# Two ways to spread PEER gates over an expert table: indirect accumulating DMAs for the first 128 tokens, one-hot products for the other 128

## The chip, the cores and the metric

The kernel runs on one core of one Trainium2 chip. The metric is device time in microseconds (us), the median of several executions. TensorE (PE in the profile) multiplies, VectorE (DVE) and ScalarE (ACT) do elementwise work, GpSimd (POOL) does elementwise work and issues DMAs of its own, and SyncE (SP) issues most DMAs. Weight loads of TensorE stand as PEld beside its products.

## The reference

The program runs a two-layer hybrid block (feed-forward, mixer, feed-forward) and then a second two-layer block (mixer, PEER) on 256 tokens of width 1024. The change is in PEER. Its core:

```python
q = (xt @ wq).reshape(T, 8, 2, 128)
s1 = einsum('thd,nd->thn', q[:, :, 0], k1); s2 = einsum('thd,nd->thn', q[:, :, 1], k2)
v1, i1 = top_k(s1, 16); v2, i2 = top_k(s2, 16)
cand = (v1[..., :, None] + v2[..., None, :]).reshape(T, 8, 256)
cidx = (i1[..., :, None] * 128 + i2[..., None, :]).reshape(T, 8, 256)
sc, pos = top_k(cand, 16)
eidx = take_along_axis(cidx, pos, axis=-1)        # 8 x 16 experts of a token
gate = softmax(sc, axis=-1)                        # per head
out[t] = sum over (h, k) of gate * gelu(u_tab[eidx] . x[t]) * v_tab[eidx]
```

There are 128 x 128 = 16,384 experts. Of a token's 128 choices two heads can name the same expert, and then both gates count.

## The kernel before

Weights come in units of 512 KB (128 partitions x 1024 floats). SP loads each into one of three slots of `ring`. ACT copies a unit to the rounded high part (`wsp`, line 435), and DVE subtracts to get the low part (line 438); three products of high and low parts stand for one full-precision product. POOL can make the low part in DVE's place (line 661). Semaphores order everything: a load waits for the low part three units back, a high part for the product three units back (`unit_done`), a product for its low part (`low_done`).

PEER of each layer gathers no rows. It computes all 16,384 activations for all 256 tokens and weights them with a dense table of gates, zero where an expert isn't chosen:

- Stage "U": `U_FIRST` = 62 of the 128 units of `u_tab`, each one product of 24 matmuls (line 688). ACT's gelu puts each into `arena`, and SP copies it out to `acts_dram`. In the meantime DVE selects: per token block b and head, `top16` on two score rows of 128, the 256 pair sums, `top16` on these, then the look-up of the chosen indices, and the softmax with ACT's exponential. DVE does nothing else in this stage, so POOL makes the low parts of `POOL_LOWS` = 60 units.
- Stage "selT": indices and gates of both blocks are transposed on TensorE.
- Stage "U2": the remaining 66 units. Behind each, from the second on, one group of four tokens: DVE writes one-hot rows for both index halves (line 2428) and multiplies the gates in (line 2437), TensorE multiplies the one-hots (eight matmuls, line 1285) into a 128 x 128 table of gates for each token, and ACT moves that to `arena`. `GROUPS` = 64 groups cover 256 tokens.
- Stage "V": `arena` holds the gates, and the activations come back from DRAM (`back`, four buffers, line 508). DVE multiplies them in (line 2455), ACT and DVE split the result (lines 1702 and 2466), and TensorE accumulates it against 128 units of `v_tab` (12 matmuls each, line 752). Before its first unit stand eleven matmuls whose result isn't used (`busy_bank`, line 678).

The order of each engine's instructions is written out by hand; there is no scheduler. `h` is saved to DRAM before the selection and comes back on POOL's queue after the last group (line 663), with the rows of the layer norm (lines 596 and 597).

Of the kernel before, what the change touches and what calls it, by code (L numbers as in the profile page):

```python
# [13 lines left out]
F32 = mybir.dt.float32  # L14
# [7 lines left out]
P = 128  # L22
# [20 lines left out]
U_FIRST = 62  # L43
POOL_LOWS = 60
SPILLED = 126
OH_SLOTS = 3
GATE_SCALE = 2.0 ** 15
GROUPS = T // 4
# [14 lines left out]
Q_N = Q_K1 + 256  # L63
# [18 lines left out]
PEER_STAGES = [("xT", 8, 0), ("tt", 16, 16), ("score", 4, 0), ("U", U_FIRST, U_FIRST), ("selT", 2, 0),  # L82
# [28 lines left out]
def build_program(nc, x, stream, consts, consts1, levels, p1, p2, swt, wa, wgu, rows1, rows2, rows3, out):  # L111
    ctx = ExitStack()
    with ctx:
# [28 lines left out]
        selT = at("selT", place + 8192 + 4 * 1280, [P, 4, T], F16)  # L142
# [7 lines left out]
        acts = at("acts", place, [P, 4, T])  # L150
# [145 lines left out]
        gates = arena[:, :].rearrange("p (j t) -> p j t", j=NKEYS)  # L296
# [23 lines left out]
        acts_dram = nc.dram_tensor("acts_dram", (NKEYS, P, T), F32, kind="Internal").ap()  # L320
# [8 lines left out]
        gated_last = sem("gated_last")  # L329
# [75 lines left out]
        def spills(slot):  # L405

            return len([j for j in range(U_FIRST, SPILLED) if j % 4 == slot])
# [62 lines left out]
        def _(sp):  # L470
# [24 lines left out]
            def act_out(U, j, q, it=0):  # L495

                U.freed(sp, q, (UNITS_BODY // 4) * it)
                if j < U_FIRST:
                    sp.dma_start(acts_dram[bass.ds(it * UNITS_BODY + j, 1)].rearrange("a p t -> p (a t)"),
                                 arena[:, bass.ds(it * (UNITS_BODY * T) + j * T, T)]).then_inc(acts_out, 16)  # L500
                else:
                    sp.dma_start(acts_dram[j], acts[:, j % 4, :]).then_inc(acts_slot[j % 4], 16)

            def act_back(l, j, it=0):

                if j >= 4:
                    sp.wait_ge(gated, SPILLED * l + j - 3 + it * UNITS_BODY)
                sp.dma_start(back[j % 4], acts_dram[bass.ds(it * UNITS_BODY + j, 1)].rearrange("a p t -> p (a t)"))\
# [3 lines left out]
            for l in range(DEPTH):  # L512
# [4 lines left out]
                with sp.Fori(0, full) as it:  # L517
                    for q in range(UNITS_BODY):
                        load(U.u + ahead + q, it, UNITS_BODY)
                        act_out(U, q, q, it)  # L520
                for q in range(full * UNITS_BODY, SPILLED):
                    load(U.u + ahead + q)
                    if q < U_FIRST:
                        act_out(U, q, q)
                    else:
                        act_out(U2, q, q - U_FIRST)
# [7 lines left out]
                sp.wait_ge(unit_done, V.u)  # L534
                act_back(l, 2)
# [2102 lines left out]
```

## Time and profile before

| | us |
|---|---|
| median of 3 runs | 3037.62 (3034.58 to 3039.28) |
| the profiled execution, its own time | 3034.38 |
| its span | 3032.6 |
| PE busy in it | 2990.2 (99%) |
| DVE busy | 2162.4 (71%) |
| ACT busy | 1493.2 (49%) |
| POOL busy | 416.6 (14%) |

Busy time is the sum over an engine's instructions. Some matmul records can be missing from a trace, and matmuls overlap in their pipeline, so of TensorE the distance from one group's start to the next's is read rather than durations. The 1.8 us between the span and the execution's own time lie outside the traced instructions.

### The profile page before, as it was taken

What the parts mean: (1) busy time and instruction counts of PE and PEld (TensorE: products, weight loads), DVE (VectorE), ACT (ScalarE), POOL (GpSimd) and SP (SyncE); (2) the same over time, 40 slices, a digit from 0 to 9 for tenths busy, and PEclk for the clock granted to TensorE, in tenths of its full rate; (3) what the DMA queues carried; (4) which work ended last, traced back from release to release, by engine and by line L of the source; (5) the groups of instructions that cost most, each with busy time, mean ns of one, the idle gap of its engine ahead of it and who ended that gap; (6) DMA issues with size and microseconds to landing.
All of it is one profiled execution on the core that took longest, in us unless ns stands there. A gap on an engine that the chain in (4) does not pass through costs nothing.

```text
span 3032.6 us, 55438 instructions
## 1 busy us (share of the span) xinstructions
PE 2990.2 (99%) x19048; PEld 2669.8 (88%) x19048; DVE 2162.4 (71%) x3762; ACT 1493.2 (49%) x2358; POOL 416.6 (14%) x246
## 2 busy tenths in 40 slices
PE   8999999999999999999999999999999999999998
PEld 7889888888898888899999988888899999988887
DVE  6677576766756667659777677776759967767776
ACT  4455444444645444444455555555444455545554
POOL 0001000000011002028800000001118810000000
PEclk9999999999999999999999999999999999999999
DMA  6543255555423554457766677775447776677775
GB/s 226 187 162 122 91 166 187 168 190 188 140 98 125 187 187 143 165 176 226 227 199 195 214 244 242 241 242 180 164 157 226 225 210 197 194 243 241 241 240 189
DMA packets 213017, 579.47 MB, mean 191 GB/s; under 512 B 23744, under 2 KB 88544, under 8 KB 212368
## 3 DMA queue, kind: packets, MB, share of 16 engines
q1 hardware_dynamic: 209504, 563.67, 58.2%
q0 software_dynamic: 3376, 13.94, 1.5%
q8 instruction: 90, 1.47, 0.2%
q14 instruction: 47, 0.39, 0.0%
HBM read 541.34 MB, written 36.18 MB: 190 GB/s over the span
## 4 chain that ended last, share of the span: by engine, by line
PE 91%; DVE 4%; ACT 2%; issue 2%; DMA 1%; POOL 0%; SPq 0%; ACTq 0%; DVEq 0%
PE acc L752 32%; PE work L688 31%; PE work L698 9%; PE work L700 4%; PE acc L1151 3%; PE acc L816 3%; PE acc L1285 2%; DVE wsp L438 1%; ACT wsp L435 1%; PE work L1185 1%; PE work L953 1%; PE work L967 1%; ACT scratch L1365 1%; PE work L1073 0%; DVE xsp L1773 0%
## 5 line engine op out<-in xcount | busy, mean ns | idle before, releaser
L438 DVE TENSOR_TENSOR wsp<-ring,wsp 128x1024 fp32r<-128x1024 f32 x824 | 1004.1, 1227 | 491.3 <-ACT wsp L435 490.5
L435 ACT ACTIVATE wsp<-ring 128x1024 fp32r<-128x1024 f32 x944 | 984.5, 1052 | 553.2 <-PE work L688 325.9
L688 PE MATMUL work<-xsp,wsp 128*128 128x256 f32 x7872 | 986.6, 286 | 2.0 <-DVE xsp L1776 2.0
L688 PEld LDWEIGHTS work<-xsp,wsp 128*128 128x128 f32 x7872 | 959.3, 193 | 4.8 <-DVE xsp L1776 2.4
L752 PE MATMUL acc<-wsp,hsp 128*128 128x512 f32 x4128 | 955.9, 390 | 6.4 <-issue 3.9
L752 PEld LDWEIGHTS acc<-wsp,hsp 128*128 128x128 f32 x4128 | 769.4, 188 | 170.3 <-issue 6.2
L698 PE MATMUL work<-xsp,wsp 128*128 128x512 f32 x1408 | 501.4, 399 | 7.1 <-DVE xsp L1773 5.4
L700 PE MATMUL work<-xsp,wsp 128*128 128x256 f32 x1408 | 395.1, 281 | 0.0
L698 PEld LDWEIGHTS work<-xsp,wsp 128*128 128x128 f32 x1408 | 264.5, 188 | 74.0 <-DVE xsp L1773 6.5
L661 POOL TENSOR_TENSOR wsp<-ring,wsp 128x1024 fp32r<-128x1024 f32 x120 | 305.9, 2557 | 156.8 <-ACT wsp L435 156.4
L1702 ACT ACTIVATE hsp<-arena 128x256 fp32r (+1 forms) x256 | 107.1, 419 | 354.4 <-PE acc L752 339.5
L700 PEld LDWEIGHTS work<-xsp,wsp 128*128 128x128 f32 x1408 | 265.9, 189 | 3.1
L563 POOL TENSOR_TENSOR st<-st,mhalf 128x1 f32<-128x1 f32 x24 | 20.5, 861 | 1573.5 <-DVE st L1793 803.9
L2428 DVE TENSOR_TENSOR one_hots<-iota,selT 128x512 f16<-128x512 f16 x256 | 97.1, 422 | 98.1 <-PE acc L1285 98.0
L2466 DVE TENSOR_TENSOR hsp<-arena,hsp 128x256 fp32r<-128x256 f32 x256 | 108.8, 425 | 57.1 <-ACT hsp L1702 57.1
L1400 ACT ACTIVATE hsp<-scratch 128x256 fp32r<-128x256 f32 x88 | 36.8, 418 | 218.3 <-DVE scratch L1866 218.3
L1392 ACT ACTIVATE scratch<-scratch 128x256 f32<-128x256 f32 x88 | 36.8, 418 | 186.5 <-DVE scratch L1856 186.5
L2455 DVE TENSOR_TENSOR arena<-arena,back 128x256 f32 (+1 forms) x252 | 105.2, 418 | 15.3 <-DMA back<-acts_dram 15.3
L2437 DVE TENSOR_TENSOR one_hots<-one_hots,selT 128x512 f16<-128x512 f16 x256 | 96.6, 419 | 0.0
L816 PE MATMUL acc<-wsp,xsp 128*128 128x512 f32 x384 | 96.0, 399 | 0.0
L1151 PE MATMUL acc<-wsp,xsp 128*128 128x512 f32 x384 | 94.0, 397 | 0.0
L1151 PEld LDWEIGHTS acc<-wsp,xsp 128*128 128x128 f32 x384 | 70.3, 188 | 15.4
(341 smaller groups left out, 2290.2 us busy)
## 6 DMA issues: line engine op xcount, KB each, us to landing
ring<-in_stream SPq DMA_DIRECT2D x944, 512.0 KB, 3.4
back<-acts_dram SPq DMA_DIRECT2D x252, 128.0 KB, 3.1
acts_dram<-acts SPq DMA_DIRECT2D x128, 128.0 KB, 3.6
acts_dram<-arena SPq DMA_DIRECT2D x124, 128.0 KB, 4.0
rows_sb<-in_rows POOLq DMA_DIRECT2D x10, 512.0 KB, 7.0
h_saved_dram<-h POOLq DMA_DIRECT2D x2, 1024.0 KB, 5.0
h<-h_saved_dram POOLq DMA_DIRECT2D x2, 1024.0 KB, 6.8
scratch<-in_levels POOLq DMA_DIRECT2D x3, 448.0 KB, 4.5
```

The costliest lines, as they stand in the source:

```text
L435: self.eng.activation(dst[:, 0, :], src, ACT.Copy).then_inc(high_done, 1)
L438: self.eng.tensor_tensor(dst[:, 1, :], src, dst[:, 0, :].bitcast(F32), ALU.subtract)\
L661: pool.tensor_tensor(dst[:, 1, :], ring[:, n % RING, :], dst[:, 0, :].bitcast(F32), ALU.subtract) .then_inc(low_done, 1)
L688: mm = pe.matmul(out_, lhsT=w[:, a, 128 * c:128 * c + 128], rhs=xsp[:, b, c, :], start=(c == 0 and n == 0), stop=(c == DC - 1 and n == 2))
L698: pe.matmul(out_, lhsT=w[:, 0, 128 * c:128 * c + 128], rhs=xcs[:, c, :, :].rearrange("p s t -> p (s t)"), start=(c == 0), stop=False)
L700: mm = pe.matmul(out_[:, 0:T], lhsT=w[:, 1, 128 * c:128 * c + 128], rhs=xsp[:, 0, c, :], start=False, stop=(c == DC - 1))
L752: mm = pe.matmul(ACC[2 * b + n][:, :], lhsT=act[:, pa, 128 * b:128 * b + 128], rhs=w[:, pw, 512 * n:512 * n + 512], start=(first and m == ...
L816: mm = pe.matmul(ACC[2 * (g % 2) + b][:, :], lhsT=xsp[:, px, c, 128 * b:128 * b + 128], rhs=w[:, pw, 512 * cc:512 * cc + 512], start=(c == ...
L1151: mm = pe.matmul(ACC[2 * (g % 2) + b][:, :], lhsT=xsp[:, px, c, 128 * b:128 * b + 128], rhs=w[:, pw, 512 * cc:512 * cc + 512], start=(c == ...
L1702: act.activation(hsp[:, j % 2, 0, :], arena[:, bass.ds(it * (6 * T) + j * T, T)], ACT.Copy)\
L2455: tt(a, a, back[j % 4], ALU.mult).then_inc(gated, 1)
L2466: tt(hsp[:, j % 2, 1, :], arena[:, bass.ds(it * (12 * T) + j * T, T)], hsp[:, j % 2, 0, :].bitcast(F32), ALU.subtract).then_inc(act_low, 1)
```

## The change

`U_FIRST` becomes 92, `POOL_LOWS` 18, `GROUPS` 32. `acts_dram` is replaced by a DRAM table for each layer, `second_dram`, of 128 x 128 x 256 floats. Of each unit's 256 columns the last 128 get the second block's activations; the first 128 get the first block's gates:

- In the mixer of the first block POOL clears the first block's half with 16 DMAs per layer, each 128 x 8 x 128 floats.
- DVE works out the position of each of the first block's choices (`spots`), and POOL adds the gates there with 128 indirect DMAs per layer, one for each head and rank, 128 single floats each. After the 16 of a head it waits until they have landed.
- The first block's activations stay in `arena`, the second block's go to `second_dram`. The second block's gates are made with one-hots as before, 32 groups behind units 92 to 123, and stand in `arena`. What comes back in stage V is therefore gates for the first block and activations for the second, and the same product serves both.
- The selection is done in three parts (four heads of the first block, its other four, the second block), with low parts of weights between them from unit 21 on.
- The last units of U2 have no group, `busy_bank` is gone, and gates and stages for V's first units stand between the last units of U2.

```diff
-U_FIRST = 62
-POOL_LOWS = 60
-SPILLED = 126
+U_FIRST = 92
+POOL_LOWS = 18
+EXP_AT = (19, 39, 76)
+ZEROED = 16
-GROUPS = T // 4
+GROUPS = P // 4
+ROUND = 16 * TOPK
...
+            to_clear = second_dram[l].rearrange("(r k p t) o -> r p k (t o)", r=ZEROED, p=P, t=T)
+            for r in range(ZEROED):
+                pool.dma_start(to_clear[r][:, :, 0:P], back0[:, 0:P].unsqueeze(1).broadcast_to([P, NKEYS // ZEROED, P]))\
+                    .then_inc(zeroed, 16)
...
+                pool.wait_ge(zeroed, 16 * ZEROED * (l + 1))
+                for i in range(PH):
+                    if i % (PH // 2) == 0:
+                        pool.wait_ge(ev("sel_ready"), 3 * l + i // (PH // 2) + 1)
+                    if PH * l + i:
+                        pool.wait_ge(scattered, ROUND * (PH * l + i))
+                    for n in range(TOPK * i, TOPK * i + TOPK):
+                        pool.indirect_dma_start(out=second_dram[l], in_=selv[:, 0, 2, n:n + 1], in_offset=None,
+                                                out_offset=bass.IndirectOffsetOnAxis(spots[:, n:n + 1], 0),
+                                                compute_op=ALU.add).then_inc(scattered, 16)
+                pool.wait_ge(scattered, ROUND * PH * (l + 1))
                 pool.wait_ge(g_done, GROUPS * (l + 1))
                 pool.dma_start(h, saved).then_inc(h_back, 16)
+                for s in range(4):
+                    pool.wait_ge(acts_slot[s], 16 * (l + 1) * spills(s))
                 load_rows(rows2[2 * l + 2, 0], rows2[2 * l + 2, 1])
...
-                    if q == SPILLED - 1:
+                    if q == NKEYS - 6:
                         sp.wait_ge(acts_out, 16 * U_FIRST * (l + 1))
-                        sp.wait_ge(ev("sel_ready"), NB * (l + 1))
-                        act_back(l, 0)
-                        act_back(l, 1)
+                        sp.wait_ge(scattered, ROUND * PH * (l + 1))
+                        second_back(l, 0)
+                        second_back(l, 1)
+                for q in range(NKEYS - 2, NKEYS):
+                    act_out(U2, l, q, q - U_FIRST)
+                sp.wait_ge(unit_done, V.u)
+                second_back(l, 2)
+                second_back(l, 3)
+                load(U.u + ahead + NKEYS - 2)
+                load(U.u + ahead + NKEYS - 1)
                 for s in range(4):
                     sp.wait_ge(acts_slot[s], 16 * (l + 1) * spills(s))
...
                 G = Group(part, "V")
-                busy_bank(G, 0, 11)
                 pe.wait_ge(g_moved, GROUPS * (l + 1))
...
-                    U2.free(act.activation(acts[:, q % 4, :], U2.bank(i)[:, 0:T], ACT.Gelu), i)
+                    act.activation(arena[:, q * T:q * T + P], U2.bank(i)[:, 0:P], ACT.Gelu)
+                    U2.free(act.activation(acts[:, q % 4, :], U2.bank(i)[:, P:T], ACT.Gelu), i)
+                    if q == NKEYS - 2:
+                        stage(0)
...
                 split.next = U.u + 3 + POOL_LOWS
                 dve.wait_ge(low_done, split.next)
+                for i in range(PH // 2, PH):
+                    for m in range(2):
+                        low_next()
+                        first_choice(0, i, m)
+                    if i == PH // 2:
+                        gates_of(0, 0, PH // 2)
...
+                for i in range(PH // 2, PH):
+                    low_next()
+                    second_choice(0, i, low_next if i % 2 else None)
+                low_next()
+                places(PH // 2, PH // 2)
+                for m in range(2):
+                    low_next()
+                    look_up(0, PH // 2, PH // 2, m, lambda: None)
+                spots_of(PH // 2, PH // 2)
+                less_the_first(0, PH // 2, PH // 2)
```

On DVE the selection of the first block's fifth head began in the kernel before without a low part between its instructions (its `top16` follows the last of the fourth head's). Now the first half ends with the spots, and from there each `top16` has a low part of a weight ahead of it (line 444 of the changed kernel is line 438 of before). The rows of the changed kernel at the end of the first half:

```order
L2452 COPY gmx<-rows_sb 128x4
L2453 TENSOR_TENSOR rows_sb<-rows_sb,gmx 128x64
L2469 SCALAR_TENSOR_TENSOR rows_sb<-rows_sb 128x64
L2470 TENSOR_SCALAR spots<-rows_sb,pr_75 128x64
L444 TENSOR_TENSOR wsp<-ring,wsp 128x1024
L2380 MAX topv<-acc 128x8
L2381 MAX_INDEX topi<-topv,acc 128x8
L2382 MATCH_REPLACE rows_sb<-topv,acc 128x128
L2385 MAX topv<-rows_sb 128x8
L2386 MAX_INDEX topi<-topv,rows_sb 128x8
L444 TENSOR_TENSOR wsp<-ring,wsp 128x1024
L2380 MAX topv<-acc 128x8
```

In the kernel before the first block's selection ended like this, and the second block's followed with no low part:

```order
L2391 COPY gmx<-rows_sb 128x8
L2392 TENSOR_TENSOR rows_sb<-rows_sb,gmx 128x128
L2345 MAX topv<-scores 128x8
L2346 MAX_INDEX topi<-topv,scores 128x8
L2347 MATCH_REPLACE rows_sb<-topv,scores 128x128
```

So low parts of weights have moved in between the selection's instructions on DVE.

On TensorE, at the end of U2 in the kernel before (line 688 is a unit's product, 1285 a group's, 678 the eleven unused matmuls, 752 stage V):

```order
L1285 MATMUL acc<-one_hots 128x128 [waits g_moved,oh_ready]
L1285 MATMUL acc<-one_hots 128x128 x7
L688 MATMUL work<-xsp,wsp 128x256 [waits low_done,bank_free3]
L688 MATMUL work<-xsp,wsp 128x256 x23
L678 MATMUL work<-xsp 128x512 [waits bank_free0]
L678 MATMUL work<-xsp 128x512 x10
L752 MATMUL acc<-wsp,hsp 128x512 [waits low_done,act_low,g_moved]
```

And in the changed kernel (714, 1310 and 778 are the same three lines):

```order
L1310 MATMUL acc<-one_hots 128x128 [waits g_moved,oh_ready]
L1310 MATMUL acc<-one_hots 128x128 x7
L714 MATMUL work<-xsp,wsp 128x256 [waits low_done,bank_free0]
L714 MATMUL work<-xsp,wsp 128x256 x23
L714 MATMUL work<-xsp,wsp 128x256 [waits low_done,bank_free1]
L714 MATMUL work<-xsp,wsp 128x256 x23
L714 MATMUL work<-xsp,wsp 128x256 [waits low_done,bank_free2]
L714 MATMUL work<-xsp,wsp 128x256 x23
L778 MATMUL acc<-wsp,hsp 128x512 [waits low_done,act_low,g_moved]
```

Three units now lie between the last group and stage V, and the unused matmuls are gone.

On POOL, the end of the low parts and the scatters of a layer (the last rows are h and the norm's rows coming back):

```order
L674 TENSOR_TENSOR wsp<-ring,wsp 128x1024 [waits high_done]
L682 DMA second_dram<-rows_sb,spots 4194304x1 [waits sel_ready,zeroed]
L682 DMA second_dram<-rows_sb,spots 4194304x1 x15
L682 DMA second_dram<-rows_sb,spots 4194304x1 [waits scattered]
L682 DMA second_dram<-rows_sb,spots 4194304x1 [waits scattered,sel_ready]
L687 DMA h<-h_saved_dram 128x2048 [waits g_done,scattered]
L608 DMA rows_sb<-in_rows 128x1024 [waits acts_slot2,acts_slot3,acts_slot1,acts_slot0]
```

These rows are new between the low parts and the return of h; the return now waits for the scatters too.

## Rows read from the trace of the kernel before

**Rows 1.** The page: busy time of the engines, and the group of ACT's high parts

```profile
PE 2990.2 (99%) x19048; PEld 2669.8 (88%) x19048; DVE 2162.4 (71%) x3762; ACT 1493.2 (49%) x2358; POOL 416.6 (14%) x246
...
L435 ACT ACTIVATE wsp<-ring 128x1024 fp32r<-128x1024 f32 x944 | 984.5, 1052 | 553.2 <-PE work L688 325.9
```

**Rows 2.** Chain that ended last, second layer's PEER: start, us, engine, line, instructions

```profile
2264.39 178.56 PE work L688 x1488
2442.95 0.65 PE work L1269 x6
...
2449.83 2.92 PE work L688 x24
2452.76 0.48 PE acc L1285 x8
...
2666.96 2.52 PE work L678 x11
2669.48 3.35 issue
2672.83 348.00 PE acc L752 x1527
```

**Rows 3.** Windows: PE, PEld, DVE, ACT, POOL busy, PE clock, DMA share, GB/s

```profile
303.00:351.00 48.00, 48.00 (x340) 43.02 (x339) 26.96 (x43) 21.86 (x49) 0.98 (x1) 1.00 0.26 88
2264.40:2443.00 178.60, 178.60 (x1490) 178.60 (x1490) 155.21 (x422) 84.78 (x127) 152.84 (x60) 1.00 0.76 218
```

**Rows 4.** Timeline of DVE in the second layer's selection: start, us, instruction

```profile
2265.16 0.30 DVE L2345 MAX8 topv<-acc 128x8 f32<-128x128 f32 x1 [5.29 <-ACT scores L1674]
...
2267.02 0.30 DVE L2345 MAX8 topv<-acc 128x8 f32<-128x128 f32 x1
...
2283.47 0.43 DVE L2345 MAX8 rows_sb<-rows_sb 128x8 f32<-128x256 f32 x1
...
2285.98 0.43 DVE L2345 MAX8 rows_sb<-rows_sb 128x8 f32<-128x256 f32 x1
...
2308.36 1.23 DVE L2369 TENSOR_TENSOR rows_sb<-topv 128x1024 f32<-128x1024 f32 x1
...
2401.05 0.23 DVE L2377 TENSOR_SCALAR posa<-posi 128x128 uint32<-128x128 uint32 x1
...
2406.32 1.23 DVE L2383 TENSOR_TENSOR hits<-pfa,iota 128x2048 f16<-128x2048 f16 x1
2407.59 3.31 DVE L2386 TENSOR_TENSOR hits<-hits,topf 128x2048 f16<-128x2048 f16 x1
2410.93 2.29 DVE L2388 TENSOR_REDUCE rows_sb<-hits 128x128 f32<-128x2048 f16 x1
```

**Rows 5.** Timeline of DVE in U2: a low part and what follows it

```profile
2447.30 1.22 DVE L438 TENSOR_TENSOR wsp<-ring,wsp 128x1024 fp32r<-128x1024 f32 x1
2448.44 0.75 DVE L2428 TENSOR_TENSOR one_hots<-iota,selT 128x512 f16<-128x512 f16 x2
```

**Rows 6.** Timeline of POOL: issues, a low part, the idle time in the mixer; one DVE row

```profile
2093.07 0.59 POOL L625 DMA_DIRECT2D scratch<-in_wa  x1
2094.19 0.96 POOL L627 DMA_DIRECT2D scratch<-in_levels  x1
...
2268.45 2.40 POOL L661 TENSOR_TENSOR wsp<-ring,wsp 128x1024 fp32r<-128x1024 f32 x1 [58.76 <-ACT wsp L435]
...
351.22 1.64 POOL L563 TENSOR_TENSOR scratch<-scratch,mhalf 128x8 f32<-128x8 f32 x1 [47.24 <-DVE scratch L2128]
...
2093.82 1.28 DVE L2203 SCALAR_TENSOR_TENSOR h<-h,st,rows_sb 128x1024 f32<-128x1024 f32 x1
```

**Rows 7.** DMA issues: the page, then 2400 to 2670 us; KB each, us to landing

```profile
back<-acts_dram SPq DMA_DIRECT2D x252, 128.0 KB, 3.1
...
rows_sb<-in_rows POOLq DMA_DIRECT2D x2, 512.0 KB, 8.4
back<-acts_dram SPq DMA_DIRECT2D x4, 128.0 KB, 7.1
```

More of the change, by code:

```diff
@@ L405, in spills @@
         def spills(slot):
[L407 removed]
+            return len([j for j in range(U_FIRST, NKEYS) if j % 4 == slot])
         class Chain:
@@ L1675, in peer @@
                 G, U2 = Group(part, "U"), Group(part, "U2")
-                with act.Fori(0, U_FIRST // UNITS_BODY) as it:
-                    for q in range(UNITS_BODY):
-                        split.one(G.u + q + 3, it, UNITS_BODY)
-                        G.ready_unit(act, q, it * UNITS_BODY)
-                        G.free(act.activation(arena[:, bass.ds(it * (UNITS_BODY * T) + q * T, T)],
-                                              G.bank(q)[:, 0:T], ACT.Gelu), q)
-                split.next = G.u + U_FIRST // UNITS_BODY * UNITS_BODY + 3
@@ new lines, in exponentials, with activate_all @@
+                def exponentials(n, g):
+                    act.wait_ge(ev("smx_ready"), 3 * l + n + 1)
+                    act.activation(g, g, ACT.Exp).then_inc(ev("smx_exp"), 1)
+                def activate_all(first, last):
+                    rounds = (last - first) // UNITS_BODY
+                    with act.Fori(0, rounds) as it:
+                        for q in range(first, first + UNITS_BODY):
+                            activate(q, it)
+                    for q in range(first + rounds * UNITS_BODY, last):
+                        activate(q)
@@ L2347, in top16 @@
                 step(dve.match_replace(tmp, vals[:, 0:8], src, LOWEST))
+                if between is not None:
+                    between()
                 step(dve.max(vals[:, 8:16], tmp))
@@ new lines, in peer @@
+                for half in range(2):
+                    low_next()
+                    pair_sums(half)
+                    for i in range(PH // 2 * half, PH // 2 * (half + 1)):
+                        low_next()
+                        second_choice(1, i, low_next if i % 2 else None)
+                    if half == 0:
+                        for i in range(PH // 2, PH):
+                            for m in range(2):
+                                low_next()
+                                first_choice(1, i, m)
@@ L2470, in peer @@
                 gate(0)
-                for j in range(SPILLED, NKEYS):
-                    gate_last(j)
+                split.upto(V.u - 1)
+                gate(1)
+                split.upto(V.u)
                 low(0)
-                gate(1)
                 split.upto(V.u + 1)
                 low(1)
+                for q in range(NKEYS - 4, NKEYS):
+                    U2.freed(dve, q - U_FIRST)
                 split.upto(V.u + 2)
```

248 lines of the change are left out of this document (139 added, 109 removed).

## The prediction

> **What bounds the kernel now.** I read the page's busy times first: TensorE is busy for 99% of the span and every other engine for 71% or less [rows 1]. Then the chain that ended last, through the second layer's PEER: stage U is one unbroken piece of 62 products in 178.56 us, 2.88 us a unit; in U2 a product and its group take 2.92 + 0.48 = 3.40 us; then come 2.52 us of unused matmuls and 3.35 us in which TensorE waits; stage V is again unbroken, 348.00 us for 128 units [rows 2]. So in PEER nearly every microsecond is TensorE's own work. A gain must take matmuls away or close the 5.87 us ahead of V; a loss comes from whatever makes TensorE wait for a weight's low part. The two layers run the same program, so I work out one and double.
>
> **What it removes.** 32 of 64 groups go. A unit with a group takes 3.40 us, one without 2.88, so a layer saves 32 x 0.52 = 16.6 us [rows 2]: **33.3 us**. Half of the six transposes (0.65 us) goes: **0.6 us** for both layers [rows 2].
>
> **The opening of V.** 5.87 us go if V can start where U2 ends. Unit 0 should: its gate, high and low part are now made during the last three units, which have no group. What comes late is SP's queue. Its `back` loads 2 and 3 stand behind the copying out of unit 127, whose gelu ACT can do only after unit 127's end, T, and after a high part of 1.05 us [rows 1]: I estimate their issue at T + 2.5. They land 3.1 us later if undisturbed [rows 7], DVE multiplies at 5.6, and unit 2 starts near T + 6.9 instead of T + 5.4. The next `back` loads wait until unit 127's activations have landed (about T + 6), just when POOL's rows of the norm, which wait for the same, start: in the kernel before such a crowd made `back` loads take 7.1 us and the rows 8.4 [rows 7]. I add 1.8 us. The opening then costs 3.3 in place of 5.87, which saves 2.6 a layer, **5.1 us**; bounds 0 (the crowd costs all of it back) and 11.7.
>
> **The selection with low parts between.** This is the new tight place. Before, POOL made 60 low parts while DVE selected [rows 3]; now POOL makes 18 and DVE makes 58 of the rest between selections (units 21 to 78). TensorE takes 58 x 2.88 = 167.0 us for them. DVE needs, start to start: a `top16` of 128 columns 1.86 us, of 256 columns 2.51, pair sums 1.26, a look-up of a full block twice (1.26 + 1.26 + 2.32) = 9.7, small instructions about 0.26 [rows 4]. For the product of hits the trace has only 3.31 us, beside POOL's low parts, which are over by then; I take the 1.23 of the equally large comparison ahead of it that ran free [rows 4]. The first block's second half: 8 x 1.86 + 1.26 + 4 x 2.51 + 4.9 + 15 x 0.26 = 35.0. The second block up to its exponential: 16 x 1.86 + 2.5 + 8 x 2.51 + 9.7 + 7 x 0.26 = 63.9. The low parts: 58 x 1.14, the distance to the next instruction [rows 5], = 66.1. Sum 165.0 against 167.0: DVE keeps up by 2 us in 167. A low part can be ready 2 x 2.88 - 1.05 - 1.23 = 3.5 us ahead, and no more, so what is gained in easy stretches isn't kept. The worst stretch is the end of the first block (two half look-ups of 3.5 us each with their low part, then spots, softmax and eight steps of 3.00 us against 2.88), about 4.2 us behind: a stall near 1 us a layer if nothing disturbs DVE. Everything that does disturb it lies on the path. The lower bound is 0. For the upper, the product of hits that met a POOL instruction ran 2.1 us over [rows 4]; eight such meetings are 17 us a layer. A direct DMA issue did not slow DVE (1.28 us beside it, two operands in SBUF) [rows 6], so I stay near the low end: 4 us a layer, **8 us lost**.
>
> The row of 3.31 against 1.23 shows that DVE and POOL can block each other. The Trainium skill ("SBUF — State Buffer", "Who interferes with whom") says that a VectorE instruction with two SBUF inputs contends with a GpSimd instruction that reads SBUF. The trace agrees for POOL's low parts, and shows none of it for direct DMAs; no row has an indirect DMA, which reads its positions from SBUF. By that rule the loss would go towards the upper bound.
>
> **Scatters.** 128 indirect DMAs a layer on POOL's queue. Their cost is in no row. POOL holds a direct DMA of 128 rows for 0.59 us and one of 896 pieces for 0.96 [rows 6]; the longest POOL instruction of the stage is 2.40. The first half of the gates is ready some 62 us into stage U (18 low parts by POOL end at 55). They must have landed when SP comes to its turn 122, where the loads of V's weights queue behind that wait, at about 92 x 2.88 + 32 x 3.40 = 373 us. That leaves 311 us, less 7 waits between heads of about 4 us (a small `back` load takes 3.1): 2.2 us a scatter. I take about 1 us, nearest to the direct issues: nothing on the path. The cover is TensorE's work of the stage; without it each 0.1 us more a scatter would cost 13 us a layer. POOL has no other work there.
>
> **Clearing.** 16 DMAs of 1024 pieces a layer, at about 1 us of issue each [rows 6], 16 us in the 47 us in which POOL is idle in the mixer [rows 6]. 8 MB beside 88 GB/s at a share of 0.26 [rows 3] fits in the same time at the 218 GB/s seen in stage U. Nothing on the path; each microsecond beyond 47 would hold up the mixer's next root, which DVE waits for.
>
> **Other edits at nothing.** ACT's gelu split in two and its table loads (ACT is busy for 85 of 179 us [rows 3]); 64 KB of each unit go out instead of 128.
>
> **Sum**, on the profiled execution's own 3034.4: 3034.4 - 33.3 - 0.6 - 5.1 + 8 = 3003.4. That execution was 3.2 us under the median of its runs; halfway, I forecast 3005.
>
> **Rivals.** (a) *Scatters late*: each holds POOL for longer than 2.2 us. At 2.40, the row of a full POOL instruction, they end at 62 + 128 x 2.40 + 28 = 397, 24 us late, 48 for both layers: 3051, slower. From 2.33 us a scatter the gain is gone. For it: 16,384 single floats, each a read and a write in DRAM, while the DMA engines are at a share of 0.76 already [rows 3]; the weights share these engines. Against it: the direct issues. The Trainium skill ("GPSIMD Engine Reference", "Performance pitfalls for Q7 kernels") gives about 102 cycles for each small read command, one per gather index, that don't overlap. By its figures, an estimate, a scatter would take 128 x 102 / 1.2 GHz = 10.9 us, and the kernel would be over 2 ms slower; no row here shows it. Chance 0.17. (b) *DVE paces stage U*: at the upper bound of 17 us a layer the result is 3034.4 - 39.0 + 34 = 3029. Chance 0.15. (c) *The change does only what it says of matmuls*, and the crowd at V's opening eats the 5.1 us: 3010; it lies in the forecast's range. (d) *Clearing holds up the mixer*: at 5 us each (POOL's ring of descriptors full) 80 us against 47 idle, 33 a layer: 3070. Chance 0.04.
>
> **Numbers.** The forecast has 0.64, with a range of its own from 2995 (no stall, V opens whole) to 3020. Measurement can tell about 0.2%, 6 us. Case (b) spreads from 3020 to 3038, a third of it within 6 us of before or above. So faster 0.75, same 0.06, slower 0.19. The range reaches from 2993 to 3042, which leaves out most of (a) and (d).
>
> **What would show it.** Right: 32 groups a layer at 3.40 us, other units at 2.88; V's first unit right behind unit 127; stage U 265 us for 92 units plus at most some 5; POOL's scatters done well before the end of U2. Wrong: idle time of TensorE ahead of products in stage U, released by DVE's low parts; an SP wait at turn 122; longer low parts on DVE beside POOL's scatters; a late root in the mixer.

## The result, and the profile after

The changed kernel takes 3009.87 us (median of 6 runs, 3007.81 to 3011.87); in the same comparison the kernel before takes 3036.66 us (6 runs, 3034.21 to 3039.28). The ratio is 0.9912, with a 95% interval of 0.9899 to 0.9925: faster by 0.9%. The profiled execution took 3007.81 us; its span is 3006.0 us against 3032.6 us before, so 26.6 us went. The forecast was 3005.

The page of the changed kernel, which answers to [rows 1], and POOL's two new groups (instructions by line; busy time, mean ns of one, idle time ahead of them and what ended it):

```profile
PE 2954.7 (98%) x18508; PEld 2634.1 (88%) x18508; DVE 2130.6 (71%) x3622; ACT 1496.1 (50%) x2390; POOL 701.0 (23%) x451
```

```profile
L682 POOL DMA_INDIRECT second_dram<-rows_sb,spots x256 | 472.0, 1844 | 145.6 <-issue 88.2 <-DMA second_dram<-rows_sb,spots 38.9 <-DVE rows_sb L2463 18.5
...
L592 POOL DMA_DIRECT2D second_dram<-back x32 | 28.4, 893 | 48.9 <-issue 48.9
```

TensorE executes 540 matmuls fewer and is busy for 35.5 us less, and POOL has 284 us more to do, 256 scatters of 1.84 us each on average, without becoming the bound.

Where the 26.6 us went is read from TensorE's timeline, as the starts of the first product of U, of the first instruction behind U2 and of the first behind V (for the second layer the end of V):

| kernel, layer | U starts | U2 is over | V is over | U and U2 | from U2 to the end of V |
|---|---|---|---|---|---|
| before, first | 1333.96 | 1736.89 | 2089.60 | 402.93 | 352.71 |
| before, second | 2264.15 | 2666.80 | 3022.86 | 402.65 | 356.06 |
| after, first | 1333.75 | 1722.58 | 2077.91 | 388.83 | 355.33 |
| after, second | 2252.48 | 2641.61 | 2996.28 | 389.13 | 354.67 |

U and U2 gained 27.6 us over both layers, and the part behind them lost 1.2 us. That is 26.4 us, all in PEER; the mixers and the feed-forward stages are where they were.

In U2 the removed groups gave what [rows 2] promised. In the chain that ended last (start, us, engine, line, instructions) two units with a group still start 3.40 us apart. The 32 groups stand behind units 93 to 124; unit 92 and the last three have none.

```profile
2527.68 2.92 PE work L714 x24
...
2531.08 2.92 PE work L714 x24
```

**Stage U.** TensorE's timeline (start, us, instruction, idle time before it and what ended it) has two listed waits for DVE's low parts in each layer; these are the second layer's, and the first's are 1.16 and 0.45 us:

```profile
2366.46 6.11 PE L714 MATMUL work<-xsp,wsp 128*128 128x256 f32 x48 [1.36 <-DVE wsp L444]
2373.03 148.10 PE L714 MATMUL work<-xsp,wsp 128*128 128x256 f32 x1224 [0.45 <-DVE wsp L444]
```

DVE's timeline in the same place shows what is ahead of the late low part (L444): the end of the second half look-up, the positions (L2470) and the subtraction before the exponential, with no low part in between. Behind it come the steps of the second block's first choice, whose low parts start 2.98 to 3.0 us apart where TensorE needs one every 2.88:

```profile
2360.44 1.22 DVE L444 TENSOR_TENSOR wsp<-ring,wsp 128x1024 fp32r<-128x1024 f32 x1
2361.59 0.69 DVE L2433 TENSOR_TENSOR hits<-pfb,iota 128x1024 f16<-128x1024 f16 x1
2362.31 0.69 DVE L2436 TENSOR_TENSOR hits<-hits,topf 128x1024 f16<-128x1024 f16 x1
2363.03 1.22 DVE L2439 TENSOR_REDUCE rows_sb<-hits 128x64 f32<-128x1024 f16 x1
...
2365.19 1.22 DVE L444 TENSOR_TENSOR wsp<-ring,wsp 128x1024 fp32r<-128x1024 f32 x1
...
2374.72 1.23 DVE L444 TENSOR_TENSOR wsp<-ring,wsp 128x1024 fp32r<-128x1024 f32 x1
2377.71 1.23 DVE L444 TENSOR_TENSOR wsp<-ring,wsp 128x1024 fp32r<-128x1024 f32 x1
2380.69 1.24 DVE L444 TENSOR_TENSOR wsp<-ring,wsp 128x1024 fp32r<-128x1024 f32 x1
```

The second wait's row says how much hides in waits too short to be listed: its 1224 matmuls are 51 units, 146.9 us at 2.88, and their stretch lasts 147.9 from its start to that of the next instruction. 92 units of 2.88, 32 of 3.40, 4 more of 2.88 and the transposes' 0.25 make 385.5 us; the layers took 3.3 and 3.6 us more, about half of it in the two listed waits.

**The opening of V.** On TensorE's timeline in the first layer V starts right behind U2, and then waits three times:

```profile
1722.58 2.91 PE L778 MATMUL acc<-wsp,hsp 128*128 128x512 f32 x12
1725.96 3.06 PE L778 MATMUL acc<-wsp,hsp 128*128 128x512 f32 x12 [0.47 <-DVE hsp L2582]
1729.47 3.01 PE L778 MATMUL acc<-wsp,hsp 128*128 128x512 f32 x12 [0.46 <-DVE hsp L2582]
1736.33 28.94 PE L778 MATMUL acc<-wsp,hsp 128*128 128x512 f32 x120 [3.85 <-DVE hsp L2582]
```

SP's queue, POOL's and DVE's in the same stretch say why. SP issues `back` 2 and 3 at 1725.54 and the next three at 1727.58; POOL issues the rows of the norm at 1727.30 and 1727.88; the fifth `back` (number 4) is multiplied only at 1735.44. It took 7.7 us to land, and the two behind it 8.7 and 9.0:

```profile
1710.14 0.86 SPq L514 DMA_DIRECT2D back<-second_dram  x2
...
1725.54 0.91 SPq L514 DMA_DIRECT2D back<-second_dram  x2
1726.49 0.91 SPq L487 DMA_DIRECT2D ring<-in_stream  x2
1727.58 1.32 SPq L514 DMA_DIRECT2D back<-second_dram  x3
```

```profile
1398.77 1.80 POOL L682 DMA_INDIRECT second_dram<-rows_sb,spots  x1 [9.30 <-DVE rows_sb L2463]
...
1701.39 1.62 POOL L682 DMA_INDIRECT second_dram<-rows_sb,spots  x1 [0.30 <-issue]
1714.64 0.61 POOL L687 DMA_DIRECT2D h<-h_saved_dram  x1 [11.63 <-PE acc L1310]
1727.30 0.59 POOL L608 DMA_DIRECT2D rows_sb<-in_rows  x1 [12.05 <-DMA second_dram<-acts]
1727.88 0.54 POOL L609 DMA_DIRECT2D rows_sb<-in_rows  x1
```

```profile
1735.44 0.42 DVE L2577 TENSOR_TENSOR arena<-arena,back 128x256 f32 x1 [4.47 <-DMA back<-second_dram]
1735.78 0.42 DVE L2582 TENSOR_TENSOR hsp<-arena,hsp 128x256 fp32r<-128x256 f32 x1
```

The second of these rows is what TensorE waited for: the low part of unit 3's own activations. Unit 3 doesn't need `back` 4. It waits for it because DVE's order has the product with `back` 4 ahead of unit 3's low part (line 2577 ahead of 2582), in the kernel before as well. The other order there would be a second way to shorten this wait; no run tried it.

The same rows show how close the scatters came. The first is issued 65.0 us into stage U, the last at 1701.39, and SP's turn 122 comes at 1710.14: 128 scatters took 304 us of a window of 311. In the second layer they run from 2317.42 to 2612.2 and SP's turn comes at 2629.16.

The wait in V also costs clock. Windows of 1 us in the second layer, behind its wait of 4.04 us (length, TensorE's busy time, granted clock, share of the DMA engines, GB/s): the clock is granted at 0.50, the lower of its two levels, and the products run at half speed for some 2.5 us.

```profile
2655.00:2656.00 1.00, 1.00 (x3) 0.50 0.22 84
2656.00:2657.00 1.00, 1.00 (x4) 0.50 0.48 70
2657.00:2658.00 1.00, 1.00 (x5) 0.71 0.75 221
2658.00:2659.00 1.00, 1.00 (x6) 1.00 1.18 399
```

The kernel before had the same dip in its second layer, behind its wait of 3.35 us, although the unused matmuls stood ahead of that wait. In the first layer, where V's first wait was 0.52 us, it had none (1.00 from 1735 to 1755 us):

```profile
2675.00:2676.00 1.00, 1.00 (x4) 0.50 0.78 246
2676.00:2677.00 1.00, 1.00 (x4) 0.50 0.91 307
```

**Clearing.** POOL's timeline in the first mixer, where [rows 6] had 47.24 us of idle time:

```profile
303.52 13.31 POOL L592 DMA_DIRECT2D second_dram<-back  x15
341.58 0.89 POOL L592 DMA_DIRECT2D second_dram<-back  x1 [24.74 <-issue]
...
352.06 1.66 POOL L571 TENSOR_TENSOR scratch<-scratch,mhalf 128x8 f32<-128x8 f32 x1 [8.28 <-DVE scratch L2163]
```

Fifteen issues took 0.89 us each, and the sixteenth came 24.74 us later; in the second layer fourteen went through, and the fifteenth came 24.17 us later. POOL was back 8.28 us before the root had work, so nothing was late, but not with the margin that 16 us of issue would have left.

### The profile page after: what moved, and what is told of

The parts are those of the page before. It is cut to its first block, busy times and chain, and to the rows that moved or that the text cites. A ratio compares the mean times of both kernels' runs of the same rounds, so it can differ in the third digit from the quotient of the medians.

```text
span 3006.0 us, 54782 instructions
## 1 busy us (share of the span) xinstructions
PE 2954.7 (98%) x18508; PEld 2634.1 (88%) x18508; DVE 2130.6 (71%) x3622; ACT 1496.1 (50%) x2390; POOL 701.0 (23%) x451
## 4 chain that ended last, share of the span: by engine, by line
PE 87%; DVE 8%; ACT 2%; issue 2%; DMA 1%; POOL 1%; SPq 0%; ACTq 0%; DVEq 0%
PE acc L778 32%; PE work L714 27%; PE work L724 10%; PE work L726 5%; PE acc L1177 3%; PE acc L842 3%; DVE wsp L444 3%; ACT wsp L441 1%; PE acc L1310 1%; PE work L1211 1%; PE work L979 1%; PE work L993 1%; DMA ring<-in_stream 1%; ACT scratch L1389 1%; DMA back<-second_dram 1%
## 5 line engine op out<-in xcount | busy, mean ns | idle before, releaser
L444 DVE TENSOR_TENSOR wsp<-ring,wsp 128x1024 fp32r<-128x1024 f32 x908 | 1105.7, 1226 | 563.7 <-ACT wsp L441 559.3
L714 PE MATMUL work<-xsp,wsp 128*128 128x256 f32 x7872 | 969.9, 284 | 6.0 <-DVE wsp L444 3.4
L682 POOL DMA_INDIRECT second_dram<-rows_sb,spots x256 | 472.0, 1844 | 145.6 <-issue 88.2
L726 PE MATMUL work<-xsp,wsp 128*128 128x256 f32 x1408 | 396.2, 281 | 0.0
L674 POOL TENSOR_TENSOR wsp<-ring,wsp 128x1024 fp32r<-128x1024 f32 x36 | 89.1, 2480 | 131.2 <-ACT wsp L441 131.2
L2577 DVE TENSOR_TENSOR arena<-arena,back 128x256 f32 (+1 forms) x256 | 107.4, 419 | 16.9 <-DMA back<-second_dram 10.9
L1177 PEld LDWEIGHTS acc<-wsp,xsp 128*128 128x128 f32 x384 | 70.3, 188 | 15.3
L842 PEld LDWEIGHTS acc<-wsp,xsp 128*128 128x128 f32 x384 | 69.7, 188 | 14.5 <-issue 0.7
```

The source lines that it names most:

```text
L444: self.eng.tensor_tensor(dst[:, 1, :], src, dst[:, 0, :].bitcast(F32), ALU.subtract)\
L682: pool.indirect_dma_start(out=second_dram[l], in_=selv[:, 0, 2, n:n + 1], in_offset=None, out_offset=bass.IndirectOffsetOnAxis(spots[:, n: ...
L714: mm = pe.matmul(out_, lhsT=w[:, a, 128 * c:128 * c + 128], rhs=xsp[:, b, c, :], start=(c == 0 and n == 0), stop=(c == DC - 1 and n == 2))
L726: mm = pe.matmul(out_[:, 0:T], lhsT=w[:, 1, 128 * c:128 * c + 128], rhs=xsp[:, 0, c, :], start=False, stop=(c == DC - 1))
L842: mm = pe.matmul(ACC[2 * (g % 2) + b][:, :], lhsT=xsp[:, px, c, 128 * b:128 * b + 128], rhs=w[:, pw, 512 * cc:512 * cc + 512], start=(c == ...
L1177: mm = pe.matmul(ACC[2 * (g % 2) + b][:, :], lhsT=xsp[:, px, c, 128 * b:128 * b + 128], rhs=w[:, pw, 512 * cc:512 * cc + 512], start=(c == ...
```

## Experiments

All are edits of the changed kernel. Waits, stage lengths and clocks are those of each kernel's one profiled execution. The times of each stand beside 7 or 13 runs of the kernel before, whose medians lay between 3035.87 and 3036.99 us.

### e1_rows_later: POOL loads the norm's rows when V is under way

```diff
+                pool.wait_ge(gated, NKEYS * l + 24)
                 load_rows(rows2[2 * l + 2, 0], rows2[2 * l + 2, 1])
```

> POOL's loads of the norm's rows wait until 24 units of stage V are gated, so that they no longer run beside the back loads 4 to 6. Theory (the crowd): those back loads land in 3 to 4 us in place of 7.7 to 7.9, the wait of about 4 us before V's third or fourth unit goes, and the time falls by 3 to 4 us a layer, to about 3002 to 3003. Rival (SP's queue is late by itself, since it stands behind the copy out of unit 127): the back loads still land too late and no more than 1 us a layer is won, about 3008.

Measured: 2999.41 us (2998.91 to 3000.84), ratio 0.9877 (0.9861 to 0.9894). The rows are now issued at 1785.08. TensorE's last wait in the first layer's opening fell from 3.85 to 2.23 us, and in the second from 4.04 to 0.29. First layer, TensorE's timeline, then a window behind the wait:

```profile
1734.86 30.43 PE L779 MATMUL acc<-wsp,hsp 128*128 128x512 f32 x133 [2.23 <-DVE hsp L2583]
```

```profile
1735.00:1740.00 5.00, 5.00 (x23) 1.00 0.52 161
```

In the changed kernel the same window has a clock of 0.66. V as a whole became 3.6 and 5.1 us shorter, 5.8 of these in listed waits, and most of the rest is clock. The median fell by 10.5 us, the span by 8.0. The theory of the crowd holds, and the price of the two loads of 512 KB was above what I expected. They are not all of the crowd: without them the first layer's `back` 4 to 6 still took 6.0 to 6.1 us to land, where the expectation had 3 to 4, and TensorE still waits 2.23 us there; in the second layer they took 3.9 to 4.1 us. What else delays them in the first layer wasn't isolated.

### e2_queue_order: SP issues the later `back` loads sooner

```diff
-                for q in range(NKEYS - 2, NKEYS):
-                    act_out(U2, l, q, q - U_FIRST)
+                act_out(U2, l, NKEYS - 2, NKEYS - 2 - U_FIRST)
...
+                act_out(U2, l, NKEYS - 1, NKEYS - 1 - U_FIRST)
...
-                for s in range(4):
-                    sp.wait_ge(acts_slot[s], 16 * (l + 1) * spills(s))
```

(the wait for the slots moves behind `back` 4 to 6)

> SP loads back 2 and 3 ahead of unit 127's copy out, and back 4 to 6 without waiting for the spilled activations. Theory (the crowd): the rows still start when the activations have landed, but back 4 to 6 are then mostly through; stage V's waits fall from about 4.5 to 5.5 us to under 2, 3003. Rival (the crowd hits whichever back loads come next): the wait moves to a later unit and the time stays at 3007 to 3010.

Measured: 3009.01 us (3003.70 to 3013.93), ratio 0.9914 (0.9897 to 0.9930). The first three units of V now run without a wait; the wait moved behind them and, in the second layer, stayed as long:

```profile
2637.67 8.35 PE L778 MATMUL acc<-wsp,hsp 128*128 128x512 f32 x36
2650.24 10.08 PE L778 MATMUL acc<-wsp,hsp 128*128 128x512 f32 x36 [4.22 <-DVE hsp L2582]
```

In the first layer the same wait was 1.26 us. This profile is of the fastest of the four runs, 3003.70 us, and the slowest took 3013.93, so these waits needn't be those of the median. The median is what the rival had: the crowd hits whichever `back` loads are under way when it comes. SP's order isn't the cause.

### e9_both: both edits

> Both edits: rows of the norm later, and SP's order. If crowd and queue each hold a part, V runs at its 348 us with under 1 us of waits, and the time is 3009.9 less 4 to 5 a layer, about 3000 to 3001. If the crowd alone was the cause, it equals e1 within 1 us.

Measured: 2998.61 us (2998.28 to 3000.57), ratio 0.9875 (0.9859 to 0.9892): the same as the first edit alone, within what these runs can tell apart. Nothing is left for SP's order to give.

### e7_busy_bank: the unused matmuls are back

```diff
                 G = Group(part, "V")
+                busy_bank(G, 0, 11)
```

> The 11 unused matmuls ahead of stage V are back (2.52 us a layer), all else as changed. Theory (the rows of the norm on POOL's queue delay the back loads, and these set when V's unit 4 or 5 can start): the matmuls only fill a part of the wait of 3.85 and 4.04 us in that place, so the time is within 2 us of 3009.9. Rival (TensorE's own work sets the opening): 2.5 us a layer more, 3015.

Measured: 3006.37 us (3003.91 to 3007.48), ratio 0.9898 (0.9882 to 0.9915). The interval overlaps that of the changed kernel, so it isn't shown to be faster, though all four runs lie below the changed kernel's six; the theory had 3008 to 3012, and 5 us slower, the rival, it is not. From U2 to the end of V the layers took 354.64 and 352.49 us with the matmuls in, against 355.33 and 354.67. The wait shrank by 2.7 us in the second layer (4.04 to 1.36), as long as the matmuls are, and the clock stayed whole:

```profile
2655.00:2656.00 1.00, 1.00 (x6) 1.00 0.78 293
```

Six matmuls of V in this microsecond against three. In the first layer a wait of 2.07 us was left, and the clock was 0.81 and 0.85 in two windows of 5 us. In this opening the matmuls that the change removed cost nothing, as long as the crowd decides: taking them out gained nothing that these runs show.

### e6_look_up_twice: DVE does the first block's second look-ups twice

```diff
                     look_up(0, PH // 2, PH // 2, m, lambda: None)
+                    look_up(0, PH // 2, PH // 2, m, lambda: None)
```

> DVE does each of the two half look-ups of the first block's second half twice (same result): 2 x 2.6 us more work on DVE, beside nothing else. Theory (DVE's own sum paces stage U there, with no slack left): TensorE's waits grow by nearly all of it, 4 to 5 us a layer, about 3018 to 3020. Rival (the 3.0 and 3.4 us lost in stage U come from late loads of weights beside the scatters): under 1 us a layer, 3010 to 3012.

Measured: 3016.97 us (3013.35 to 3021.18), ratio 0.9931 (0.9914 to 0.9947), 7.1 us more than the changed kernel. The waits, listed for stage U of either layer (us in total, times, the longest), were 1.6 and 1.8 before the edit:

```profile
PE work L714 <- DVE wsp L444: 6.3, 2, 4.3
...
PE work L714 <- DVE wsp L444: 5.1, 2, 3.0
```

Two further half look-ups are 2 x 2.7 = 5.4 us of DVE's time a layer, and TensorE's listed waits are 4.7 and 3.3 us longer, three quarters of it. U and U2 as a whole became 6.4 and 5.2 us longer; the clock behind these waits was low too (0.59 in the first layer from 1455 to 1460 us, 0.66 in the second from 2380 to 2385, where the changed kernel's waits of 1.16 and 1.36 us left it at 1.00). This profile is of the slowest of the four runs, 3021.18 us; by the medians 7.1 us of the 10.8 added came through, a little less than the 8 to 10 expected, and far from the rival's 0 to 2. What is added there lies for the most part on the path.

### e5_no_scatters: one scatter a head instead of sixteen

```diff
-ROUND = 16 * TOPK
+ROUND = 16
...
-                    for n in range(TOPK * i, TOPK * i + TOPK):
+                    for n in range(TOPK * i, TOPK * i + 1):
```

(the second edit in its effect; 15 in 16 of the first block's gates are left out)

> Leaves out 15 of the 16 scatters of each head, so 15 in 16 of the gates of the first block are missing. Theory (the sum of DVE's own work sets the waits in stage U): TensorE's waits for DVE's low parts stay at 1.6 and 1.8 us, and the time stays within 3 us of the changed kernel's 3009.9, as the scatters only took POOL's time. Rival (the scatters disturb DVE or the weights' loads): the waits in stage U vanish and the time falls by 3 to 7 us, to 3003 to 3007.

Measured: 3005.61 us (3004.93 to 3006.56), ratio 0.9899 (0.9882 to 0.9915); the span is 2.9 us under the changed kernel's. The time lies in the rival's range (3003 to 3007) and not in the theory's, but the waits in stage U, which were to tell the two apart, stayed as the theory had them, 0.3 us shorter in either layer:

```profile
2365.88 6.10 PE L714 MATMUL work<-xsp,wsp 128*128 128x256 f32 x48 [1.06 <-DVE wsp L444]
```

U and U2 became 0.4 and 0.5 us shorter, so that little is what 240 scatters can have cost there. The rest lies behind U2, where the layers were 1.1 and 2.2 us shorter: V's last waits are 3.26 and 3.32 us in place of 3.85 and 4.04. Why these are shorter, when the last scatter was issued 21 and 31 us before V opened, wasn't followed up, and the intervals of the two kernels overlap.

### e3_one_more_head: a ninth round of scatters

```diff
-                for i in range(PH):
+                for i in range(PH + 1):
...
-                    for n in range(TOPK * i, TOPK * i + TOPK):
+                    for n in range(TOPK * (i % PH), TOPK * (i % PH) + TOPK):
```

(the waits on `scattered` count the ninth round too; head 0's gates are added twice)

> A ninth round of 16 scatters a layer (head 0's gates are added once more, so the output has them twice) is queued behind the eighth. Theory: after the change the scatters were done only about 4 to 7 us ahead of SP's turn 122 in the first layer and about 17 us ahead in the second; 16 more take 16 x 2.14 + about 3 = 37 us, so the loads behind turn 122 come some 30 us late in the first layer and 20 in the second. What the weights already loaded ahead cover is unknown, some 5 us: 3009.9 + 25 + 15 = about 3050, between 3040 and 3060, with TensorE idle at the end of U2 or the opening of V. Rival: the scatters' end is hidden better than this, because the weights loaded ahead of turn 122 carry TensorE further: then within 10 us of the changed kernel, 3010 to 3020.

Measured: 3043.02 us (10 runs, 3036.97 to 3051.34), ratio 1.0025 (1.0016 to 1.0035): slower than the kernel before. SP waited 39.2 us in both layers together for the scatters at its turn 122 (waits of SP's queue), and TensorE stood still one unit before V (its timeline, both layers):

```profile
SPq L535 <- DMA second_dram<-rows_sb,spots: 39.2, 2, 20.5
```

```profile
1732.82 5.33 PE L714 MATMUL work<-xsp,wsp 128*128 128x256 f32 x24 [14.57 <-DVE wsp L444]
...
2666.63 4.46 PE L714 MATMUL work<-xsp,wsp 128*128 128x256 f32 x24 [12.83 <-DVE wsp L444]
```

The weights that were loaded ahead carried TensorE over about 6 us of each of SP's waits, as expected; the time came to 33 us more, where 40 were expected. One head more, 12.5% more scatters, takes the whole gain.

### e4_clear_twice: every clearing DMA twice

```diff
-            for r in range(ZEROED):
+            for r in [*range(ZEROED), *range(ZEROED)]:
```

(the second sixteen wait until the first have landed; the wait on `zeroed` counts both)

> Every clearing DMA is issued twice (32 of 1024 pieces a layer, the second 16 behind the first 16). Theory: with the ring of descriptors full, each further one waits for an older one to land; the first 15 took 13.3 us to issue and the 16th 25, and 8.19 MB moved in about 45 us, so the second 16 hold POOL some 40 to 50 us more, against 8.3 and 8.9 us that POOL had idle ahead of the mixer's root. So about 35 us a layer: 3080, between 3060 and 3100. Rival: the root is not what the mixer waits for, or the second 16 are issued as fast as the first (13 us): then +5 us a layer or nothing, 3010 to 3020.

Measured: 3064.42 us (3060.84 to 3066.37), ratio 1.0087 (1.0071 to 1.0104), 54.5 us more. POOL's timeline in the first layer, and TensorE's behind it:

```profile
341.14 0.89 POOL L597 DMA_DIRECT2D second_dram<-back  x1 [25.13 <-issue]
345.88 12.31 POOL L597 DMA_DIRECT2D second_dram<-back  x14 [3.86 <-DMA second_dram<-back]
377.59 1.76 POOL L597 DMA_DIRECT2D second_dram<-back  x2 [19.40 <-issue]
```

```profile
389.76 1.97 PE L772 MATMUL work<-cst,scratch 128*128 128x128 f32 x8 [27.94 <-DVE scratch L2184]
```

POOL was free 37 us later, 8.3 of them were cover, and TensorE waited 27.94 us in this layer and 27.70 in the second. In the first pass the issues stop behind the fifteenth, in the second behind the fourteenth. Clearing is hidden, but its cover is almost used up.

### e10_pool_lows_15 and e12_low_sooner: two edits of stage U, on top of e9_both

```diff
-POOL_LOWS = 18
-EXP_AT = (19, 39, 76)
+POOL_LOWS = 15
+EXP_AT = (16, 36, 73)
```

> The version with the rows of the norm held back and SP's new order, and POOL makes 15 low parts at the start of stage U instead of 18 (exponentials three units sooner). DVE waited 9.12 us for POOL to finish those, so it takes up its own low parts three units, 8.6 us, sooner and the scatters begin about 9 us sooner and end about 9 us sooner. Theory (waits in stage U come from a short dense stretch of DVE's work, wherever it lies, and the scatters were hidden already): the same waits of 1.5 us a layer, the same time as without this edit, 2998.6, within 2 us. Rival (the scatters' end, at a margin of 4 to 7 us in the first layer, already delays the back loads there, which wait 2.2 us): the first layer's opening closes, 2996.

Measured: 2998.87 us (2997.88 to 3000.01), ratio 0.9873 (0.9857 to 0.9890). The scatters started 7.8 us sooner and ended 5.9 us sooner in the first layer, the listed waits of TensorE in stage U were 1.8 and 1.6 us (1.6 and 2.1 without the edit), and the time is the same.

```diff
                 for m in range(2):
                     low_next()
+                    turns = iter((low_next, int)) if m else iter((int, int))
-                    look_up(0, PH // 2, PH // 2, m, lambda: None)
+                    look_up(0, PH // 2, PH // 2, m, lambda: next(turns)())
...
-                low_next(3)
+                low_next(2)
```

> The version with the rows of the norm held back and SP's new order, and DVE makes one more low part inside the second half look-up of the first block, and one fewer behind the second block's selection. Theory (the waits of TensorE for a low part, about 1.1 and 0.45 us a layer, come from 5 us of DVE's work between two low parts there): every later low part gains 2.88 - 1.14 = 1.7 us of slack, both waits vanish, stage U to U2 takes 385.6 us, and the time falls by 3 us, from 2998.6 to 2995.6. Rival (DVE has no slack at all in the stretches behind): the waits move to a later unit, same time.

Measured: 2995.68 us (2994.50 to 2997.11), ratio 0.9864 (0.9848 to 0.9880), the fastest kernel of this study. The intervals of this ratio and of the two it is set against overlap; the 3 us are carried by the runs, of which all four lie below the lowest of the edit above (2997.88) and of e9_both (2998.28). DVE's timeline shows the low part that is now between the look-up's product and its sum, and TensorE's waits in stage U (first, then second layer) are all but gone:

```profile
2357.12 0.69 DVE L2437 TENSOR_TENSOR hits<-hits,topf 128x1024 f16<-128x1024 f16 x1
2357.85 1.23 DVE L444 TENSOR_TENSOR wsp<-ring,wsp 128x1024 fp32r<-128x1024 f32 x1
2358.99 1.21 DVE L2440 TENSOR_REDUCE rows_sb<-hits 128x64 f32<-128x1024 f16 x1
```

```profile
PE work L715 <- DVE wsp L444: 0.3, 1, 0.3
...
PE work L715 <- DVE wsp L444: 0.2, 1, 0.2
```

U and U2 took 387.17 and 387.30 us, against 389.24 and 389.60 in e9_both; the span fell by 3.3 us, since in this execution stage U began 1.5 us later. The 1.7 us a layer above 385.5 that are left are, with only 0.3 listed, waits too short to be listed; the eight steps of 2.98 us are where I look for them, but no run isolated those.

## Why the prediction was right, and where it was not

**Groups and transposes** (33.3 and 0.6 us): right. U and U2 fell by 27.6 us, which is 33.3 for the groups and 0.8 for the transposes (0.65 less 0.25 us, twice), less 6.5 us of new losses in stage U.

**The selection with low parts between** (8 us lost): right in mechanism, in place and nearly in size: 6.5 measured, where I took 4 a layer (the layers stand 3.3 and 3.6 us over the ideal sum, and those before stood 0.4 and 0.1 over theirs). The late part is the end of the first block, as the sum by durations had it, and e6_look_up_twice and e12_low_sooner show that it is DVE's own work there that decides: adding 5.4 us costs most of it, and one low part moved forward takes 4.4 us out of U and U2 over both layers. The estimate from the durations alone, about 1 us, fell short of the 3.3 and 3.6; the 4 us a layer were a choice between bounds of 0 and 17, and that they came so close is in part luck. What the estimate missed is probably the slow leak of the eight steps that take 0.1 us more than a unit, which I counted only into the sum of the worst stretch; no run isolated it. The product of hits at 1.23 us, which I had to assume, took 1.23 in the second block's look-up. The half of it (128x1024) took 0.69 us when it ran free and 2.78 beside POOL's low parts, which cost nothing, as DVE then waited 9.12 us before it could take over the low parts.

**The opening of V** (5.1 us saved): wrong. It lost 1.2 us. V without any wait takes 348.7 us from its first product to its end (both layers of e12_low_sooner, less their one wait). The kernel before took 4.0 and 7.4 us more than this from the end of U2 to the end of V, 11.4 together, and the changed kernel 6.6 and 6.0, 12.6 together; I had 11.7 and 6.6. So the half of the term that stands for the old kernel was right in sum, but by luck: I read 5.87 us from the second layer and doubled it, while in the first layer of the same trace V's first product starts 3.20 us behind U2, and the second paid 1.3 us of low clock on top. Saying "the two layers run the same program" was no reason to skip the look at the other. The half for the new kernel holds the error, and it has two parts. First, the crowd was sized too small. The first steps came as written: `back` 2 and 3 issued at T + 3.0 (T + 2.5 forecast) and unit 2 at T + 6.9, exactly. Then `back` 4 landed 7.7 us after its issue, close to the 7.1 of [rows 7], and that is 3.85 us of waiting for one unit where I added 1.8. Secondly, nothing in the term stood for the clock: behind a wait of about 4 us TensorE ran at half speed for some 2.5 us, and the loss exceeds the listed waits of 4.8 and 4.3 us by 1.8 and 1.6. With the unused matmuls back, in e7_busy_bank, the second layer's wait was shorter and its clock stayed whole; the first layer's clock fell all the same, and in the kernel before the second's did too, with these matmuls in place. So their removal isn't shown to be what lowers it. e1_rows_later takes the norm's rows out of the crowd and wins 10.5 us. A crowd that eats the 5.1 us was rival (c), at 3010, and it is what happened.

**Scatters**: "nothing on the path" was right, and the price beneath it wrong. I took about 1 us each; they held POOL for 1.84 us on average (median 1.58, longest 7.85), with 0.30 us between two: 2.14, where I had put the point of decision at 2.2. The window was forecast well (62 us to 373 us into stage U; measured 65 and 376), and the scatters were "well before the end of U2" only in the second layer. In the first the last one ended at 1703.0, and the waits between heads say that landing takes 2.2 to 3.9 us more, so rival (a) was missed by 3 to 5 us. In other executions the last scatter of that layer was issued between 1695.2 and 1704.9, so this margin moves by some 10 us, and in the latest of them (e12_low_sooner) at most 1.5 us of it can have been left. That nothing lay on the path was thus right by luck. e3_one_more_head shows the cliff behind it: 16 scatters more and the kernel is slower than before. A forecast of 0.17 for (a) was too low for a price that no row showed.

The Trainium skill ("GPSIMD Engine Reference", "Performance pitfalls for Q7 kernels") has about 102 cycles for each small read command, such as one for each index of a gather; the estimate by its figures was 10.9 us a scatter, and the trace disagrees: 128 indices took a median of 1.58 us. The Trainium skill's rule on shared access ("SBUF — State Buffer", "Who interferes with whom"), as the prediction applied it to scatters, would have let them slow DVE. DVE's low parts ran at 1.21 to 1.24 us beside the scatters and without them. Some scatters take 2.4 to 2.6 us, and in the first layer seven in a row (1586.08 to 1603.36) start 2.88 us apart, the distance at which DVE's low parts, and all else that follows a unit, come there; which of these holds them up is not shown. For POOL's low parts the trace does agree (2.78 against 0.69 us for the half product of hits).

**Clearing** (nothing on the path): right, by 8.3 us instead of the 30 that the issues alone would have left, since the sixteenth issue waited 24.74 us. e4_clear_twice put 27 us a layer on the path as soon as this cover was gone, so rival (d) had its mechanism and its place right; its price, 5 us for each DMA, was reached by none of the first fourteen.

The profiled execution came out 4.4 us over the sum of 3003.4: the opening was 6.3 us dearer than its term, the losses in stage U were 1.5 us smaller, and the transposes gave 0.2 us more. The forecast stood 1.6 us over its sum and the median 2.1 us over the profiled execution, and so the total is 4.9 us off.

## What to carry to other kernels

When a stage is opened earlier, look at every transfer that the same event lets go: here two loads of 512 KB that nobody needed before V's end were released together with the small loads that TensorE was waiting for, and one wait in front of them was worth 10.5 us, about a third of what the removed groups were worth. Where one engine feeds another at nearly its rate, total up the work between two deliveries, not the total over the stage: moving one low part forward was worth 3 us. And read a wait in each layer before doubling it, and what the clock does behind it; a hidden piece of work is only as safe as its margin, which one longer run of it measures at once.

## What the runs showed of the hardware

An indirect accumulating DMA of 128 single floats holds POOL for 1.54 us at the least, in the median 1.58, with 0.30 us to the next; one of 7.85 us fell on the start of DVE's one-hots, in the first layer only. When all scatters of a head are issued, the next head's start 2.2 to 3.9 us later if they wait for them to land. POOL's queue takes fourteen or fifteen DMAs of 1024 pieces at 0.89 us each and then stands for 24 to 25 us while 8 MB move (share of the DMA engines 0.80 at 256 GB/s, 303 to 351 us, against 0.26 before). The granted clock behind a wait in V, over 5 us: 0.66 after 3.85 us, 0.74 after 4.04, 0.66 after 4.22 (e2_queue_order), 0.69 after 3.26 and 1.00 after 3.32 (both e5_no_scatters), 1.00 after 2.23 (e1_rows_later), 0.81 after 2.07 (e7_busy_bank), 0.75 after 3.35 (the kernel before, second layer). The length of the wait alone doesn't tell which it will be, and what else decides stays open.
